# Rotary of the retention heads moved off TensorE, and rows of the output projection moved into the end of an attention

## What is computed

```python
proj = h @ w_in
mixed = concatenate([retention_mixer(ret_cols, ...), dsa_mixer(dsa_cols, ...), dilated_mixer(dil_cols)])
x = x + mixed @ w_out
x = x + square(relu(rms_norm(x) @ w_up)) @ w_down
```

```python
q, k = rotary(q, pos), rotary(k, pos)      # [x1*cos - x2*sin, x2*cos + x1*sin], x1 and x2 the halves of a head
o = retention_chunkwise(q, k, v)           # sum over s <= t of gamma^(t-s) (q_t . k_s) v_s
o = (o - mean(o)) * rsqrt(var(o) + eps) * norm_w * silu(g)
```

## Time and profile before

| | |
|---|---|
| median of three runs | 2446.7 us |
| the profiled execution, device time | 2444.1 us |
| its span | 2442.1 us |
| TensorE busy | 2384.3 us, 98% |
| VectorE, ScalarE, GpSimd busy | 1042.1, 955.4, 1028.2 us (43%, 39%, 42%) |
| DMA | 212.36 MB, 87 GB/s mean |
| mean granted clock of TensorE | 0.994 |

### The profile page before, as it was taken

The page is one execution under the profiler, slowest core; times in us unless marked ns, Lnnn a source line. Parts: engine busy times, 40 slices in busy tenths (PEclk is TensorE's granted clock), DMA queues, the critical chain, the costliest instruction groups (busy, mean ns, idle before and its releaser), DMA issues.

```text
span 2442.1 us, 29458 instructions
## 1 busy us (share of the span) xinstructions
PE 2384.3 (98%) x11848; PEld 1906.6 (78%) x11848; DVE 1042.1 (43%) x1922; ACT 955.4 (39%) x1329; POOL 1028.2 (42%) x815
## 2 busy tenths in 40 slices
PE   8999999999999989999999989999999999999997
PEld 6777588888877767888888769888889768788887
DVE  4677541121337776211225445422224768322224
ACT  5345452232343445432335355422224485422223
POOL 4433144444444232444444453444444334444442
PEclk9999999999999999999999999999999999999999
DMA  5212023232232121322323212223323312322331
GB/s 164 77 52 96 26 95 104 87 104 87 83 108 87 36 96 36 103 94 96 104 86 117 86 35 70 87 87 104 104 87 104 104 51 88 104 86 87 104 104 52
DMA packets 138279, 212.36 MB, mean 87 GB/s; under 512 B 7456, under 2 KB 65952, under 8 KB 137888
## 3 DMA queue, kind: packets, MB, share of 16 engines
q1 hardware_dynamic: 138144, 210.48, 26.5%
HBM read 208.36 MB, written 2.10 MB: 86 GB/s over the span
## 4 chain that ended last, share of the span: by engine, by line
PE 54%; DVE 4%; ACT 3%; POOL 1%; issue 1%; DMA 0%; ACTq 0%; SPq 0%; DVEq 0%
PE ps L312 47%; PE ps L337 2%; POOL w_lo L275 1%; PE ps L1823 1%; PE ps L842 1%; ACT w_hi L266 1%; DVE h_lo L569 1%; PE ps L865 1%; PE ps L823 1%; DVE tmp_both L684 0%; DVE x L689 0%; DVE ssum L465 0%; ACT L493 0%; PE ps L486 0%; PE ps L1295 0%
## 5 line engine op out<-in xcount | busy, mean ns | idle before, releaser
L275 POOL TENSOR_TENSOR w_lo<-raw,w_hi 128x512 fp32r<-128x512 f32 (+1 forms) x776 | 994.4, 1315 | 1371.8 <-ACT w_hi L266 1371.4
L312 PE MATMUL ps<-h_hi,w_hi 128*128 128x512 f32 x1696 | 682.5, 402 | 13.1 <-POOL w_lo L275 13.1
L312 PE MATMUL ps<-h_hi,w_lo 128*128 128x512 f32 x1696 | 663.4, 391 | 0.0
L312 PE MATMUL ps<-h_lo,w_hi 128*128 128x512 f32 x1696 | 663.0, 391 | 0.0
L266 ACT ACTIVATE w_hi<-raw 128x2048 fp32r<-128x2048 f32 (+2 forms) x196 | 361.3, 1854 | 584.7 <-PE ps L312 457.6
L312 PE MATMUL ps<-hid_hi,w_hi 128*128 128x512 f32 x992 | 390.6, 394 | 4.9 <-DVE hid_lo L936 3.8
L312 PEld LDWEIGHTS ps<-h_hi,w_hi 128*128 128x128 f32 x1696 | 318.6, 188 | 97.0 <-issue 17.9
L312 PE MATMUL ps<-hid_hi,w_lo 128*128 128x512 f32 x992 | 387.5, 391 | 0.0
L312 PE MATMUL ps<-hid_lo,w_hi 128*128 128x512 f32 x992 | 387.5, 391 | 0.0
L312 PEld LDWEIGHTS ps<-h_lo,w_hi 128*128 128x128 f32 x1696 | 318.3, 188 | 69.9 <-issue 5.2
L312 PEld LDWEIGHTS ps<-h_hi,w_lo 128*128 128x128 f32 x1696 | 317.9, 187 | 70.2 <-issue 0.2
(11 more groups left out here) (304 smaller groups left out, 2780.9 us busy)
## 6 DMA issues: line engine op xcount, KB each, us to landing
raw<-in_w_up SPq DMA_DIRECT2D x32, 1024.0 KB, 5.4
raw<-in_w_down SPq DMA_DIRECT2D x32, 1024.0 KB, 5.1
raw<-in_ffn_w_gate SPq DMA_DIRECT2D x44, 512.0 KB, 3.9
raw<-in_ffn_w_up SPq DMA_DIRECT2D x44, 512.0 KB, 4.9
raw<-in_w_in SPq DMA_DIRECT2D x20, 1024.0 KB, 5.0
raw<-in_ffn_w_down SPq DMA_DIRECT2D x20, 1024.0 KB, 5.0
raw<-in_w_out SPq DMA_DIRECT2D x8, 1024.0 KB, 5.3
raw<-in_ev_w_in SPq DMA_DIRECT2D x8, 1024.0 KB, 5.4
```

Source lines behind the costliest of these rows:

```text
L275: pool.tensor_tensor(w_lo[slot.buf][:, k, 0:slot.width], raw[r][:, k, 0:slot.width], w_hi[slot.buf][:, k, 0:slot.width].bitcast(F32), ALU. ...
L312: mm = pe.matmul(o, lh, rh, start=first and q == 0, stop=last and q == 2, skip_group_check=True)
```

## The change

The rotation no longer uses TensorE. SP copies q and k with the halves of each head exchanged, by eight transfers within SBUF of 32 partitions each (`swap`), GpSimd multiplies them by the sines (which now carry the sign) and q and k in place by the cosines, and DVE adds the two. Cosines, sines and the swapped copies lie in the space of the dilated q, whose early blocks are free by then; only the decay stays in `h_hi`. `out_a` runs 12 of its 16 tiles in the last four steps of the dilated attention, and the other four in step 0 of DSA. Retention begins at step 4 and not 6, `out_b` takes ten steps from 12 on, the group norm's means move to other banks and two steps earlier, while its Ln and Exp stay in step 16. The 96 tiles beside the dilated attention take 34 steps and not 36, and five rounds of the top-k search are taken early.

```diff
-            dil_pace = Pace(3 * 32, 0, dil.steps() - 3)
-            out_a, out_b = Pace(16, 0, 3), Pace(16, 16, 7)
-            ROT, RET, GN = 4, 6, 15
+            dil_pace = Pace(3 * 32, 0, dil.steps() - 5)
+            out_a, out_b = Pace(12, dil.steps() - 4, 4), Pace(16, 12, 10)
+            ROT, RET, GN, LN = 1, 4, 13, 16
...
+                load_slots(sp, s0 + 14)
+                sp.wait_ge(*at("s_ready", 8))
+                sg["rot_in"].by(sp.dma_start(cos_t[:], a["rtab"][:, T_COS:T_COS + S]), 16)
+                sg["rot_in"].by(sp.dma_start(sin_t[:], a["rtab"][:, T_SIN:T_SIN + S]), 16)
+                load_slots(sp, pl.s_mix + 1)
+                sp.wait_ge(*at("s_ready", 24))
+                sp.wait_ge(sems["bank_free"], BANKS + HALF * (pl.retqk + 1))
+                for i in range(2):
+                    for r in range(0, P, HD // 2):
+                        o = r ^ (HD // 2)
+                        sg["ret_swap"].by(sp.dma_start(swap[i][r:r + HD // 2, :, :],
+                                                       retqk[o:o + HD // 2, 2 * i:2 * i + 2, :]), 16)
                 load_slots(sp, pl.s_mix + 2)
                 sp.wait_ge(sems["bank_ready"], HALF * (pl.retv + 1))
-                sg["consts"].by(sp.dma_start(rtab[:], a["rtab"]), 16)
+                sg["decay_in"].by(sp.dma_start(decay[:], a["rtab"][:, T_DECAY:]), 16)
...
-                stream_lo(pool, pl.s_mix + 2)
-                pool.wait_ge(*at("consts", 16 * 3))
-                pool.wait_ge(sems["bank_free"], BANKS + HALF * (pl.retqk + 1))
+                stream_lo(pool, pl.s_mix)
+                pool.wait_ge(*at("rot_in", 32))
+                pool.wait_ge(*at("ret_swap", 16 * 8))
                 for j in range(4):
-                    sg["ret_cos"].by(pool.tensor_tensor(st_b[j][:], retqk[:, j, :], rtab[:, T_COS:T_COS + S], ALU.mult))
+                    o = swap[j // 2][:, j % 2, :]
+                    sg["ret_sin"].by(pool.tensor_tensor(o, o, sin_t[:], ALU.mult))
+                stream_lo(pool, pl.s_mix + 1)
+                for j in range(4):
+                    sg["ret_cos"].by(pool.tensor_tensor(retqk[:, j, :], retqk[:, j, :], cos_t[:], ALU.mult))
...
-                dil.tensor(pe, lambda i: dil_pace.emit(i, tiles))
-                tiles_a = tiles_of(pl.out_a, FEAT, hid_hi, hid_lo, k0=KT)
+                tiles_a = tiles_of(pl.out_a, FEAT, hid_hi, hid_lo, k0=KT, ready=("mix_lo", base["mix_lo"] + 1 - KT))
+
+                def beside_dil(i):
+                    dil_pace.emit(i, tiles)
+                    out_a.emit(i, tiles_a)
+
+                dil.tensor(pe, beside_dil)
...
                     if i == 0:
-                        pe.wait_ge(*at("mix_lo", 4))
-                    out_a.emit(i, tiles_a)
-                    if i == ROT:
+                        rest(tiles_a)
+                    if i == RET:
                         pe.wait_ge(sems["bank_free"], BANKS + HALF * (pl.out_a + 1))
-                    if ROT <= i < ROT + 2:
-                        for j in (2 * (i - ROT), 2 * (i - ROT) + 1):
-                            sg["ret_rot"].by(pe.matmul(ps[:, 4 + j, :], rot_m, retqk[:, j, :], start=True, stop=True))
...
-                        if i == GN + 1:
+                        if i == LN:
                             act.wait_ge(*at("gn_var", j + 1))
                             alink(act, act.activation(st_b[j][:], ps[:, 6 + j, :], ACT.Ln, bias=eps_c))
...
-                        take(1)
+                        take(2 if i % 4 == 1 and i < 20 else 1)
...
-                    for m in range(4):
-                        if out_a.step_of(4 * (m + 1)) + 1 == i:
+                    if ROT <= i < ROT + 2:
+                        for m in (2 * (i - ROT), 2 * (i - ROT) + 1):
                             add_out(pl.out_a, m, m)
-                    if i == ROT:
-                        dve.wait_ge(*at("consts", 16 * 3))
-                    if ROT <= i < ROT + 2:
                         for j in (2 * (i - ROT), 2 * (i - ROT) + 1):
-                            dve.wait_ge(*at("ret_rot", j + 1))
-                            link(dve, dve.tensor_tensor(gn[j % 2][:], ps[:, 4 + j, :], rtab[:, T_SIN:T_SIN + S], ALU.mult))
+                            dve.wait_ge(*at("ret_sin", j + 1))
                             dve.wait_ge(*at("ret_cos", j + 1))
-                            sg["ret_rotd"].by(dve.tensor_tensor(retqk[:, j, :], gn[j % 2][:], st_b[j][:], ALU.add))
-                            dve.wait_ge(*at("ret_rotd", j + 1))
+                            sg["ret_rotd"].by(dve.tensor_tensor(retqk[:, j, :], swap[j // 2][:, j % 2, :],
+                                                                retqk[:, j, :], ALU.add))
```

More of the change, by code:

```diff
@@ L37 @@
 HALF = 4
-T_IDENT, T_ONES, T_MEAN, T_ROT, T_LOGC, T_CAUSAL, T_POOL = 0, 128, 256, 384, 512, 1024, 1536
-T_SHARED = 1600
+T_IDENT, T_ONES, T_MEAN, T_LOGC, T_CAUSAL, T_POOL = 0, 128, 256, 384, 896, 1408
+T_SHARED = 1472
 T_COS, T_SIN, T_DECAY = 0, 512, 1024
@@ L58, in shape_tables @@
     t[:, T_MEAN:T_MEAN + P] = half / HD
-    for m in range(P):
-        if m % HD < HD // 2:
-            t[m + HD // 2, T_ROT + m] = -1.0
-        else:
-            t[m - HD // 2, T_ROT + m] = 1.0
     dist = q - (np.arange(S)[None] - (S - P))
@@ L77, in shape_tables @@
     r[:, T_COS:T_COS + S] = np.cos(ang.astype(np.float64))
-    r[:, T_SIN:T_SIN + S] = np.sin(ang.astype(np.float64))
+    sign = np.where(np.arange(P) % HD < HD // 2, -1.0, 1.0)[:, None]
+    r[:, T_SIN:T_SIN + S] = np.sin(ang.astype(np.float64)) * sign
     diff = np.arange(S)[None] - q
@@ L1146, in build @@
         rl = p_t
-        rtab = place("rtab", [P, T_RET], where=t_off["h_hi"])
+        decay = place("decay", [P, RET_H * S], where=t_off["h_hi"])
+        cos_t = place("cos_t", [P, S], where=t_off["dil_q_hi"])
+        sin_t = place("sin_t", [P, S], where=t_off["dil_q_lo"])
+        swap = [place(f"swap{i}", [P, 2, S], where=t_off[n] + 2048) for i, n in enumerate(("dil_q_hi", "dil_q_lo"))]
         st_b = [place(f"ret_st{i}", [P, S], where=t_off["h_lo"] + i * 2048) for i in range(4)]
@@ L1309, in retention @@
                             pe.wait_ge(*at("gn_in", j + 1))
-                            sg["gn_mean"].by(pe.matmul(ps[:, 4 + j, :], mean_m, gn[j][:], start=True, stop=True))
+                            sg["gn_mean"].by(pe.matmul(ps[:, 6 + j, :], mean_m, gn[j][:], start=True, stop=True))
                         if i == GN + 1:
@@ L1400, in beside_dil @@
                             sg["dq_high"].by(act.activation(dsaq_hi[:, m, :], dsaq[:, m, :], ACT.Copy))
-                    if i == len(dil.units) + 1:
+                    if i == len(dil.units) + 3:
                         act.wait_ge(sems["bank_free"], BANKS + HALF * (pl.dsaq + 1))
@@ L1418, in retention @@
                     for j in range(2):
-                        if i == GN + 1:
+                        if i == LN:
                             sg["gn_rstd"].by(act.activation(st_b[j][:], st_b[j][:], ACT.Exp, scale=-0.5))
-                        if i == GN + 2:
+                        if i == LN + 1:
                             act.wait_ge(*at("gn_out", j + 1))
@@ L1605, in retention @@
                             sg["ret_p"].by(dve.tensor_tensor(st_b[u % 4][:, 0:w], ps[:, 4 + u % 2, 0:w],
[L1606 removed]
+                                                             decay[:, h * S:h * S + w], ALU.mult))
                     if i == GN - 1:
@@ L1614, in retention @@
                             dve.wait_ge(*at("gn_mean", j + 1))
-                            sg["gn_c"].by(dve.tensor_tensor(gn[j][:], gn[j][:], ps[:, 4 + j, :], ALU.subtract))
-                    if i == GN + 1:
+                            sg["gn_c"].by(dve.tensor_tensor(gn[j][:], gn[j][:], ps[:, 6 + j, :], ALU.subtract))
+                    if i == LN:
                         for j in range(2):
```

7 lines of the change are left out of this document (3 added, 4 removed).

## The result

| | before | changed |
|---|---|---|
| median, us | 2445.06 (2442.18 to 2447.24, 20 runs) | 2448.81 (2444.69 to 2453.4, 20 runs) |
| ratio | 1 | 1.0015 [1.0008, 1.0021] |
| profiled span, us | 2442.1 | 2448.1 |

The change made the kernel slower by 3.7 us. I had forecast 2.5 us faster, so the direction is wrong. The median of 2448.8 us lies just inside my own range (2439.5 to 2449), but only because the kernel before came out at 2445.06 us and not at the 2446.7 us that I started from: as a difference the range was -7.2 to +2.3 us. The change of 0.15% is within the band of 0.2% either way, to which I had given 0.47.

What follows compares the result with a forecast made beforehand. TensorE, busy 98% of the span, was taken as the bound. Terms -7.5 - 3.9 - 5.6 + 6.0 + 4.0 = -7.0 us, with clock +4.5 giving -2.5: 2446.7 to 2444.2 us; own range 2439.5 to 2449.

Steps and rivals of the forecast that it cites:

- The waits at head and tail: TensorE's waits around DSA: 3.9 and 5.6 us go, 6.0 us come at its head, 4.0 us net at the norm.
- The rotation, -7.5 us: TensorE's rotation matmuls in DSA go, 2 x 1.88 us a layer, 7.5 us over both, all of it counting.
- Waits that go, -3.9 and -5.6 us: TensorE's 1.93 us wait at DSA's start goes (3.9 us); waits of 0.32, 0.33 and 2.18 us go too (5.6 us).
- Head of DSA, 3.0 us a layer: Scores of step 4 wait 2.6 us for VectorE's mask of unit 3, plus 0.4 us in small gaps.
- Group norm, 3.8 us a layer: In out_b, TensorE idles 3.8 us for ScalarE's Ln and Exp; net 2.0 us a layer with neighbouring waits.
- my 0.2 us for `rb`: Behind the norm's Exp, VectorE's rb takes 3.0 us, four tiles cover 2.8, so the turned sums wait 0.2 us.
- Two gaps of 0.9 and 1.2 us late in the dilated attention may shrink or stay; I leave them: TensorE gaps late in the dilated attention, left out of the sum.
- VectorE has slack: Early top-k rounds lengthen five VectorE steps by about 1.2 us at no cost; without slack, 0.2 to 1 us each.
- The clock, +4.5 us: TensorE's clock drops four times in the changed stretches, not twice, costing 9.4 us: 4.5 us more than before.
- Exclusion at the adds, 0 us: VectorE's rotary adds were to miss GpSimd's split: 0 us, 6.4 us kept for the range; meeting it had chance 0.07.
- The transfer within SBUF: Swapped q and k copy ahead of GpSimd's products: 5.6 us taken, up to 23 us possible, covered, costed at nothing.
- the rival of the slow transfer: At 23 us the transfer makes out_a's tiles 10 us late a layer, some 2460 us; chance 0.06.

Runs made afterwards that it cites:

- Experiment 8: Changed kernel at 36 steps for the 96 tiles, with out_b back in steps 16 to 22 and the means in step 15: 2439.6 us, 0.9978 against before.
- experiment 4: Changed kernel with the 96 tiles beside the dilated attention taking 36 steps again, not 34: 2443.8 us, 0.9998 against before.
- experiment 5: Changed kernel, 34 steps kept, with ScalarE's high part of the second dsaq tile ahead of the w_hi split: 2446.2 us, 1.0009 against before.
- experiment 3: Changed kernel with one top-k round in each step as before: 2446.7 us, 1.0008 against before.

## Why the prediction was wrong

In the profiled executions the terms came out as follows. The rotation took 7.5 us, as forecast. The waits at head and tail, which I had at +0.5 us in all, came to -0.4. The gaps of the dilated attention, which I had at 0, came to +5.2. The clock, which I had at +4.5, came to +6.8. Outside these are 1.9 us, 1.2 of them at the start. Together they are +6.0 us. The sign is wrong by the third term and, less, by the fourth.

**The rotation, -7.5 us: right.** No L1286, and the rotation alone gained 5.7 us net.

**Waits that go, -3.9 and -5.6 us: right.** None of the four is left.

**Head of DSA, 3.0 us a layer: right in size, its parts not.** It was 3.4 us in both. That the total came near was luck. I had one gap of 2.6 us for the mask behind eight operations. It is two, 1.34 us for ScalarE's copy between the two turns and 1.55 us for the mask. I had let the turns pass with their copy by 4.8 us and not counted that TensorE has nothing else while the copy runs. With the adds away from there, the second fell to 0.35 us.

**Group norm, 3.8 us a layer: right to 0.03 us.** The waits of 0.97 and 1.07 us went as said, a gap of 0.35 us with them, and of my 0.2 us for `rb` nothing was seen: net 1.4 us a layer where I had 2.0. Experiment 8 got 0.9 of it back.

**"Two gaps of 0.9 and 1.2 us late in the dilated attention may shrink or stay; I leave them": this step failed.** They and their neighbours grew by 5.2 us over both layers. I had put the pace of 34 steps in a subordinate clause ("The tile groups are cut into more pieces, a few tenths") and asked of it only what TensorE loses. It also moves ScalarE's splits, high parts and VectorE's evacuations to other steps. That is where it cost: experiment 4 shows it in the time, which falls by 4.2 us by the ratios with 3.9 us less of gaps, and experiment 5 shows how for the gap near 167 us.

**"VectorE has slack": half wrong.** The early rounds as such cost nothing in the steps where they stand, and the 1.11 us gap is not theirs. But they shift the sequence of widths, and one of 512 columns fell in front of a mask that TensorE waits for, 0.54 us a layer. By the ratios experiment 3 lies 1.7 us under the changed kernel, inside both intervals.

**The clock, +4.5 us: the term was too small, 6.8.** The count was meant as four drops of 4.7 us in the changed stretches, 18.8 us; there were five, 23.9 us, the fifth behind the gap of 2.60 us that I had not forecast. The long gap at the norm dropped it in both layers as expected, and the head in both, for 10.3 us in the first. At the head my reason was one gap of 2.6 us, and the drops came behind 1.34 and 1.55 us.

**Exclusion at the adds, 0 us: right; and yet it cost elsewhere.** The adds took 1.29 us for two. But `dsaq_lo` took 1.36 us and `hid_lo` 1.57 us beside GpSimd's work where they take 0.68 alone. The Trainium skill ("SBUF — State Buffer", the section on its two separate sides) says that a VectorE instruction with two SBUF inputs and a GpSimd instruction that reads SBUF take one shared pair of ports in turn, each for its whole length; by that rule, the trace agrees. Nor are two inputs the only case: the copy that spreads `rb`, with one, took 1.27 us at 223.34 us beside GpSimd's cosines, where its median is 0.43. I had asked it of four adds only, where every such subtraction near a split was to be asked.

**The transfer within SBUF: covered, as taken.** SP's queue and the median times from issue to landing:

```profile
201.65 5.13 SPq L1201 DMA_DIRECT2D swap<-retqk  x8
```

```profile
swap<-retqk SPq DMA_DIRECT2D x8, 128.0 KB, 2.5
```

From the first issue to the first product it was 208.98 - 201.65 = 7.3 us, where I had 5.6; the issues alone are 5.13 us of it. The sines started at 209 and not before 208 us. TensorE never waited for it, and the rival of the slow transfer falls.

What made the kernel slower was none of my rivals. A part of it, VectorE late in the dilated attention, had a price in my text (0.2 to 1 us a round without slack), but no rival and no chance.

## What to carry to other kernels

A number that sets a pace moves work on every engine that counts steps by it. Before costing it, list for each engine which two operations now share a step, and in which order. Filler (here tiles that TensorE can do at any time) taken from one place is missed there: ask of each piece that is moved what wait it had been covering, and move the cause of that wait first. Two kernels with the same sum of gaps differed by 6 us here, and the clock fell in the one and not in the other.
